# The delta-rule scan: eight of the sixteen small transfers that bring the inverted diagonal blocks back are issued by ScalarE instead of SyncE

## The reference, cut to what matters

```
lmat  = where(tril_strict, einsum(k_beta, k) * decay, 0)
t_inv = triangular_solve(eye + lmat, eye, lower=True, unit_diagonal=True)
u = t_inv @ v_beta ;  w = t_inv @ (k_beta * exp(g))
for each chunk:
    v_new = u_i - w_i @ state
    o_i   = (q_i * exp(g_i)) @ state + a_i @ v_new
    state = state * exp(g_last) + (k_i * exp(g_last - g_i))^T @ v_new
```

## Time and profile before

| what | before |
|---|---|
| device time, median of 3 runs | 2722.41 us (2721.79 to 2727.39) |
| span of the profiled execution | 2733.5 us |
| PE busy over the span | 2537.5 us, 93% |
| DVE, ACT, POOL busy | 63%, 45%, 23% |
| transfers into `x_base` | 320 of 8 KB, all issued by SP |
| transfers issued by ACT in the whole kernel | 20, none in the scan |

### The profile page before, as it was taken

The page is one execution under the profiler, slowest core; times in us unless marked ns, Lnnn a source line. Parts: engine busy times, 40 slices in busy tenths (PEclk is TensorE's granted clock), DMA queues, the critical chain, the costliest instruction groups (busy, mean ns, idle before and its releaser), DMA issues. The chain is left out here.

```text
span 2733.5 us, 45747 instructions
## 1 busy us (share of the span) xinstructions
PE 2537.5 (93%) x17286; PEld 2387.3 (87%) x17286; DVE 1709.1 (63%) x2810; ACT 1231.2 (45%) x2225; POOL 625.1 (23%) x558
## 2 busy tenths in 40 slices
PE   6999999969998999985999998989999999999999
PEld 3899999958887888884778777989999999999999
DVE  3666332146676577745988883446886664777776
ACT  4322344233433334323888883344653333545443
POOL 1000222243443343313563544332000000000000
PEclk9999999978998899975999999999999999999999
DMA  5322666343335333314111004632335551537764
GB/s 219 139 86 94 203 220 205 127 130 90 94 103 164 96 110 92 84 31 140 55 39 63 17 13 136 241 136 94 120 107 177 191 187 66 175 105 249 261 223 150
DMA packets 238032, 357.63 MB, mean 131 GB/s; under 512 B 85984, under 2 KB 161792, under 8 KB 236288
## 3 DMA queue, kind: packets, MB, share of 16 engines
q1 hardware_dynamic: 234944, 339.11, 38.0%
q10 hardware_dynamic: 2880, 15.73, 1.7%
HBM read 262.66 MB, written 92.09 MB: 130 GB/s over the span
## 5 line engine op out<-in xcount | busy, mean ns | idle before, releaser
L277 PE MATMUL proj_ps<-h_hi,w_hi 128*128 128x320 f32 x896 | 282.9, 316 | 6.0 <-DVE w_lo L575 5.6
L277 PE MATMUL proj_ps<-h_lo,w_hi 128*128 128x320 f32 x896 | 278.2, 310 | 0.0
L277 PE MATMUL proj_ps<-h_hi,w_lo 128*128 128x320 f32 x896 | 277.9, 310 | 0.0
L1079 ACT ACTIVATE x_inv<-banks_bc 128x1024 fp32r<-128x1024 f32 x120 | 122.7, 1025 | 275.3 <-PE banks_bc L1213 274.5
L2276 DVE TENSOR_TENSOR mf_up_slots<-mf_up_raw,mf_up_slots 128x512 fp32r<-128x512 f32 x198 | 137.3, 694 | 117.9 <-ACT mf_up_slots L2251 117.7
L277 PEld LDWEIGHTS proj_ps<-h_hi,w_hi 128*128 128x128 f32 x896 | 169.7, 189 | 7.1 <-DVE w_lo L575 3.3
L277 PEld LDWEIGHTS proj_ps<-h_lo,w_hi 128*128 128x128 f32 x896 | 169.7, 189 | 0.0
L277 PEld LDWEIGHTS proj_ps<-h_hi,w_lo 128*128 128x128 f32 x896 | 169.5, 189 | 0.0
L3049 PE MATMUL f_ps_b<-mf_t_r,mf_up_slots 128*128 128x320 f32 x1056 | 166.0, 309 | 3.2 <-DVE mf_sg L2964 3.2
L3049 PE MATMUL f_ps_b<-mf_t_s,mf_up_slots 128*128 128x320 f32 x1056 | 166.6, 310 | 2.0 <-PEq L2281 2.0
L3049 PE MATMUL f_ps_c<-mf_t_s,mf_up_slots 128*128 128x320 f32 x1056 | 166.3, 310 | 0.0
(11 more groups left out here) (395 smaller groups left out, 6880.5 us busy)
## 6 DMA issues: line engine op xcount, KB each, us to landing
mf_up_raw<-w_up_dram SPq DMA_DIRECT2D x33, 1024.0 KB, 5.0
w_raw<-w_in_dram SPq DMA_DIRECT2D x48, 512.0 KB, 4.3
mf_down_raw<-down_sums SPq DMA_DIRECT2D x32, 704.0 KB, 4.4
mf_down_raw<-w_down_dram SPq DMA_DIRECT2D x24, 704.0 KB, 4.5
w_ada_raw<-w_ada_dram SPq DMA_DIRECT2D x16, 1024.0 KB, 5.0
mf_w_raw<-w_mix_dram SPq DMA_DIRECT2D x30, 512.0 KB, 5.0
f_t<-mf_c SPq DMA_DIRECT2D x44, 320.0 KB, 2.4
delta_t<-delta_tile ACTq DMA_DIRECT2D x10, 1024.0 KB, 6.7
```

What stands on the lines that cost most here:

```text
L277: ins = nc.tensor.matmul(out, w(k), a(k), start=(first and n == 0 and q == 0), stop=(last and n == len(ks) - 1 and q == 2))
L1079: nc.scalar.activation(XX[:, c].rearrange("p t h i -> p t (h i)"), BC[c][:], ACT.Copy).then_inc(e["x_ready"], 1)
```

## The change

SP's `inverse_in` issues only the eight transfers of the straight copies. A new function in ACT's program issues the eight of the turned copies. It waits for the pair to be written out, and stands in ACT's turn after `decay(u + 3, 0)`, ahead of all that ACT does at the third level.

```diff
                 for b in range(8):
                     rows = slice(16 * b, 16 * b + 16)
-                    for x in range(2):
-                        sp.dma_start(XB[rows, x, :, rows].bitcast(F32), io["diag_inv"][b, :, x].rearrange("h i j -> i h j")).then_inc(e["xb_in"], 16)
+                    sp.dma_start(XB[rows, 0, :, rows].bitcast(F32), io["diag_inv"][b, :, 0].rearrange("h i j -> i h j")).then_inc(e["xb_in"], 16)
...
+            def inverse_turned_in(k):
+                act.wait_ge(e["pair_out"], 16 * (k + 1))
+                if k:
+                    act.wait_ge(e["z_ps"], z_index[k - 1, LV[0], 1] + 1)
+                else:
+                    act.wait_ge(e["xb_zero"], 1)
+                for b in range(8):
+                    rows = slice(16 * b, 16 * b + 16)
+                    act.dma_start(XB[rows, 1, :, rows].bitcast(F32), io["diag_inv"][b, :, 1].rearrange("h i j -> i h j")).then_inc(e["xb_in"], 16)
...
                     if has(u + 3) and lv in (LV[1], LV[2]):
                         decay(u + 3, lv - LV[1])
+                    if has(u + 1) and lv == LV[1]:
+                        inverse_turned_in(u + 1)
```

## The result

| | before | after |
|---|---|---|
| device time, median | 2724.9 us (2721.79 to 2728.86, 4 runs) | 2756.66 us (2752.11 to 2762.66, 4 runs) |
| span of the profiled execution | 2733.5 us | 2751.4 us |
| device time of that execution | some 2735.3 us (its span plus 1.8) | 2753.22 us |

The ratio is 1.0112, with a 95% interval of 1.0092 to 1.0133: 31.8 us lost where 18 were forecast. A second set of runs of the same kernel gave 1.0116 (1.0087 to 1.0145), its medians 28.2 us apart. The new profile gives the profiled execution's own device time, which is 1.8 us above its span. So the 11.1 us between the span of before and its median was nothing fixed: that one execution was 10 us longer than the usual one.

The account below looks back on a forecast made before the run. PE was taken as all but full, busy 28.65 of 30.3 us a turn. SP's gain -12.3, ACT's stands +20.8 and clock +9.9 gave +18.4, which put on the median 2722.4 made 2740 us, range 2710 to 2772.

Parts of the forecast that it names:

- SP's gain: Eight fewer issues free 3.7 us of SP every turn; shorter PE stands were to gain 12.3 us in all.
- The wait at the reload: Unit 9's turn: PE's 4.45 us stand before using reloaded activations was to shorten by 2, bounds 0 and 3.7.
- The 3.3 that I gave to the other waits: DVE's remaining waits for `diag_blocks`, felt by PE through `attn_t`: 3.3 us gained, bounds 0 and 10.
- the first unit's 3.3 us: First unit: PE's single 3.3 us wait for `x_base` was to vanish because the transfers land earlier.
- ACT's pace and its wait: After `decay`, ACT waits 0.4 us for the pair, then issues eight at 0.5 us each, 4.0 us.
- The stands lost: PE standing for ACT's later copies and evictions in the scan: 20.8 us lost in all.
- The plain turns: Ordinary scan turns: ACT's late copy just passes PE's need; five turns at 0.3 to 0.5, 1.7 us lost.
- The clock: Half-clock falls behind PE's stands: five of seven new stands cost 17.5 us, avoided falls return 7.6; net 9.9 lost.
- From span to median: Whole kernel: the profiled span's 11.1 us above the median was carried over, turning 2752 into 2740.
- the queues hold each other up: Rival, chance 0.1: issues on both queues take 0.93 us each and SP saves nothing; +74, 2797 us.
- Stalls without clock falls: Rival, chance 0.2: same delays in the scan, no falls following and one avoided; +4.1, 2726.5 us.
- SP's time wins: Rival, chance 0.2: ACT issues at 0.303 us, so ordinary turns lose nothing; -13.6, 2709 us.

Follow-up runs that it names:

- experiment 3: Kernel before, SP issuing all sixteen, with ACT only waiting for the written pair at the change's place and writing one number: 2726.15 us, ratio 1.0001.
- experiments 7 and 8: Kernel after, ACT's eight issues replaced by six constant copies: 2753.83 us, ratio 1.0098; kernel after, ACT issuing four and SP twelve: 2728.73 us, ratio 1.0004.
- experiment 2: Kernel after with ACT's eight issues moved behind the third level's second decay: 2707.21 us, ratio 0.9930 to the kernel before.
- the plain turns alone: Kernel after with ACT issuing the turned half only for twelve units not forecast as heavy, SP all sixteen in the other eight: 2734.39 us, ratio 1.0026.
- experiment 1: Kernel after with SyncE's eight alone: ACT's eight left out, PE waiting for eight, part of the computation missing: 2708.71 us, ratio 0.9934.
- experiment 4: Kernel before, SP issuing all sixteen, plus eight extra ACT issues from a weight into a spare tile: 2795.21 us, ratio 1.0258.

## Why the forecast went right and wrong

The direction and the cause were right, the size was not: 18.4 us forecast, 31.8 measured (25 to 36). Step by step:

- **SP's gain.** 12.3 us in stands and 7.6 in avoided falls of the clock, 19.9 in all; SyncE's eight alone gained 18. Right as a sum, with some luck: the rest fell by 9 us, in the traces (1181.6, the mean of three, to 1172.6) as in the runs, and the clock's part by 10 in the runs, so one part was too high and the other too low. The parts: DVE's wait for `diag_blocks` fell from 23.2 to 9.2 us, and unit 7's long stand is gone. The wait at the reload is 4.45, 6.11 and 3.90 in the three traces with SyncE's sixteen, 4.19 with SyncE's eight alone, and 3.24 and 3.37 in the kernel after, so a gain of 1 to 2 is all that can be said where I took 2. The 3.3 that I gave to the other waits by way of `attn_t` doesn't show: PE waited 24.7 us for it, against 24.5. In the kernel after, the first unit's 3.3 us were not gained, since ACT's eviction took the place of the transfer; that cost was missing in my sum.
- **ACT's pace and its wait.** 0.5 us forecast, 0.47 measured, and in several turns 0.59. The wait costs nothing (experiment 3). Right.
- **The stands lost.** 20.8 us forecast. The traces give 21.7 (1172.6 to 1194.4, the mean of two), the runs 22.5. Right as a sum, and experiments 7 and 8 bear out the mechanism: cover is used up and just passed. Two slips in the working change little: by its own numbers the end of the scan comes to 5.2 and 2.2 instead of 5.3 and 2.3, and unit 14's 1.4 does not lie between 1.7 and 4.7. The plain turns were taken too low. I gave 1.7 us to five of them; single ones stood 1.2 to 1.3 us (units 6, 8 and 11, in one or the other trace). I had read ACT's duty off one undisturbed turn, although SP's rows show batches of issues at 8.7 us beside those at 7.43.
- **The clock: the step that failed.** "I take that five of the seven are followed by a fall of 3.5 us each, 17.5", less 7.6, net 9.9. The runs give up to 27 for the first and up to 10 for the second, net 17 where 9.9 was forecast (13.2 in the scan by PE's busy time alone): of the 13.4 us by which the forecast fell short, some 7 are the clock's and some 5 are in the stands (13.5 net where I had 20.8 less 12.3). And the clock term was not only too small but in part in the wrong place. Of the seven stands only three, of 3.0 to 4.2 us in the two traces of the kernel after, are followed by falls of their own, in the turns of units 5, 15 and 16; those of 1.4 to 1.7 us (units 4, 7 and 10) are not, and unit 14's did not come. Half of PE's busy time in these three falls is 9 us in one trace and 10 in the other, where I had 17.5 for five. Other falls between 860 and 1047 became longer or are in one trace and not in the next. In the traces the net is 17 as well, and 3.6 of it lie behind the scan, where nothing was changed. Of the falls that I called avoided, the one at 828 is in all three traces with SyncE's sixteen and not in the two of the kernel after, while that at 930 is in one of them only: it belonged to an execution, not to the kernel. So what the other two thirds of the 27 follow from stays open.
- **From span to median.** I carried the 11.1 us between span and median over. The span was forecast at 2752 and came as 2751.4, which is luck; the median was forecast at 2740 and came as 2756.7. The profiled execution of before was 10 us longer than the median, that of after 3.4 shorter. Runs of the unchanged kernel lie up to 28 us apart, so the distance of one execution from its median could not be carried to another kernel.
- **The rivals.** That the queues hold each other up is out (3.64 and 3.75 us side by side). Stalls without clock falls is out too, by the 17 us net. That SP's time wins holds only where ACT has cover, at the late place. The Trainium skill (DMA: Bandwidth & Descriptors, section Issuing engines are not separate DMA queues) says that the saved sequencer time is usually small beside the transfer; the runs say otherwise for these transfers: eight issues take 3.7 us and one transfer lands in 1.7, and saving them was worth 19 us where it cost nothing (experiment 2).

What is not settled: how much of the 27 us each stand's fall has, and why the plain turns alone, whose longest stand on `x_inv` is 0.9 us, have 7.7 us more clock loss than the kernel before. That the falls follow from the stands was read from the traces, not tried: no experiment filled a stand with other work.

## What to carry to other kernels

Issuing a DMA is work of the engine that issues it, and that engine's list is served in order: price it as so many issues by so many us at that very place, and ask when the next thing behind it is needed. The same eight issues cost 50 us in one place and nothing that could be measured one level later, and with half of them at the first place the time stayed that of before. Here, where TensorE is all but full, 22 us of stands and later work came with 27 us of lost clock, and one trace doesn't say how much of that belongs to which stand: compare medians for the total, and take a clock term from the granted clocks of many runs.

## What the runs showed of the hardware

- A batch of eight issues took 3.64 us on SyncE and 3.75 on ScalarE at the same time, as fast as SyncE alone. In some turns both took 4.7, and SyncE alone up to 4.87 (experiment 1). For transfers of the same shape from another source, a weight, ScalarE needed 0.64 us an issue instead of 0.47 (experiment 4).
- In the 13 traces, TensorE stood 82 times for 2.2 us or more in the scan after running at full clock, and during 81 of these stands or within 8 us behind them there were windows at half clock. Of 106 stands of 1.00 to 1.12 us, 14 had them. Between these, 48 of 71 had, but on `x_inv` only 4 of 14. How long a fall lasts differed from execution to execution at one and the same stand (6.8 us at half clock from 749 in one trace of the kernel after, 3.4 in the other).
- Executions of the kernel before spread from 2712 to 2740 us over all its runs. Half of the time at half clock in the scan spreads over 14 us between three traces of that order of work, and what is left over 2.
